# Taking q, k and v apart by tile in the latent attention's projection loop: q signals alone, and three steps change places

## The chip, the cores and the metric

The kernel runs on 1 core of one Trainium2 chip. The metric is the device time of one execution in microseconds (us). One kernel launch computes the whole model.

## The reference

Two layers over 512 tokens of width 1024. Each layer is a mixer of two attention branches, followed by a mixture of experts. The change lies in the branch with latent projections (`mla_attention`) and its hand-over to the attention loop:

```python
qb = (rmsnorm(bq, q_norm[l]) @ w_qb[l]).reshape(B, S, B_HEADS, B_NOPE_DIM + B_ROPE_DIM)
qn, qr = qb[..., :B_NOPE_DIM], qb[..., B_NOPE_DIM:]
qr = apply_rope(qr, cos[:, :, None, :], sin[:, :, None, :])
kvb = (rmsnorm(bkv, kv_norm[l]) @ w_kvb[l]).reshape(B, S, B_HEADS, B_NOPE_DIM + B_V_DIM)
kn, vb = kvb[..., :B_NOPE_DIM], kvb[..., B_NOPE_DIM:]
kr = apply_rope(bkr, cos, sin)
ob = mla_attention(qn, qr, kn, kr, vb)
gates = jax.nn.sigmoid(h @ w_gate[l] + b_gate[l])
```

`apply_rope` turns the last 32 of the 96 columns of each of the 8 heads by the angles of the token's position. `mla_attention` is a chunk-causal softmax attention over all 512 keys. The other branch, `swa_sink_attention`, is a sliding window with 2 key heads and a sink. After both, `mix = ga * (oa @ w_oa) + gb * (ob @ w_ob)` goes through `w_out` into the residual, and then 64 experts (8 groups of 8), the best 2 of the best group for each token, with D_EXPERT = 256.

## The kernel before

The program is written by hand for each engine: one block of code for SP (loads), GpSimd (POOL), ScalarE (ACT), VectorE (DVE) and TensorE (PE), and counting semaphores between them. Each engine works its own list strictly in the order written. The tokens stand in NT = 4 tiles of P = 128. The 8 PSUM banks are `ps[0]` to `ps[7]`.

A product in float32 is made of three passes (`mm3`, L1639 to L1641): the weights are split into a high part `wh` (made by ACT, L718) and a low part `wl` (made by DVE, L1120), the activations likewise. The weights come in units of up to 1 MB. `plan` lists them: units 0 to 2 and 3 to 6 are `w_in`, 7 and 8 `w_qb` (q), 9 `w_kvb` (k and v), 10 to 17 the gates (`U_G`), then `w_oa`, `w_ob`, `w_out`. `split_to(n)` on ACT and on DVE splits all units below n. SP loads a unit when its place in SBUF is free.

**The q/k/v loop** is the place of the change. On PE, for tile i (L1747 on): the product for q into banks `ps[o]` and `ps[o+1]` (18 matmuls of 384 columns), the product for k and v into `ps[o+2]` and `ps[o+3]` (12 matmuls of 512 columns), with o = 0 for even and 4 for odd tiles; then, for tile i-1, 8 transposes of q (L1780) and 8 of k (L1787) back into the same banks. Before q's product of tile i >= 2 PE waits until ACT has taken the transposed q of tile i-2 out of the banks (`qt_ev`), and before k's and v's product until DVE has taken the transposed k (`kt_ev`). The last round, i = NT, has transposes only.

- ACT, tile i: wait for the product, copy q (`qc`, L867, two), copy v (L870), then for tile i-1 copy the transposed q out (`qt`, L876, two). At i = 2 it then makes the high parts of gate unit 10 (8 instructions).
- DVE, tile i: wait for the product, copy k's part without angles (`kc`, L1291) and the shared turned part (L1293), then turn q by its angles (`rope`, L1274 to L1279, six), then for tile i-1 copy the transposed k out (`kt`, L1307, two). At i = 2 it then makes the low parts of gate unit 10 (8 instructions).

All wait for one signal a tile, which PE sets at the end of the v product:

```python
last.then_inc(S["qkv_ps" if i < NT - 1 else "unit_used"], 1)
```

PE's transposes of q of tile t wait for `q_roped`, those of k for `kn_copied`, `k_ready` and `v_copied`.

**The attention loop** follows: steps u = 0 to 63 of (query tile, head, branch). PE's step u puts out the scores of step u+1 (L1809 or L1813 for the window branch, L1818 for the latent branch), a quarter of a gate product (`gate_chunk`, from u = 1 on, L1639 to L1641, 6 matmuls), the transposes of the probabilities of step u (L1868) and the product with the values of step u-1 (L1882). DVE makes the maximum (`negm`, L1358 or L1364), ACT the exponential (L923 or L929). Before the loop ACT waits for all `kt_ev`. Before the first gate chunk PE waits for all `qt_ev` and `kt_ev`.

Of the kernel before, what the change touches and what calls it, by code (L numbers as in the profile page):

```python
# [23 lines left out]
P = 128  # L24
# [12 lines left out]
def hybrid_trunk(nc, x, positions, norm_mix, w_in, sinks, q_norm, w_qb, kv_norm, w_kvb, w_gate, b_gate,  # L37
# [3 lines left out]
    NT, KD = T // P, D // P  # L41
# [3 lines left out]
    HEADS = AH  # L45
    ROPE = IN_W - AQ - 2 * A_KV * A_DIM - QR - KVR
    HALF = ROPE // 2
# [79 lines left out]
    with ctx:  # L127
# [209 lines left out]

        block = ctx.enter_context(nc.Block())

        def dist_of(t):  # L340
# [355 lines left out]
        def _(act):  # L696
# [52 lines left out]
            for l in range(L):  # L749
# [107 lines left out]
                for i in range(NT + 1):  # L857
                    if i < NT:
                        o = 4 * (i % 2)
                        product_ready(act, "qkv_ps", i, NT, U_QKV)  # L860
                        if i >= 2:
                            act.wait_ge(S["qk_ps"], 2 * (i - 1))
                        if i == 0:
                            act.wait_ge(S["rstd2_done"], 1)
                        hh = HEADS // 2
                        for n in range(2):
                            nc.scalar.activation(qc[i % 2][:, n * hh:(n + 1) * hh, :].rearrange("p h d -> p (h d)"),  # L867
                                                 ps[o + n][:, 0:hh * QD], ACT.Copy, scale=rstd2[:, 0, i:i + 1]
                                                 ).then_inc(S["q_copied"], 1)
                        nc.scalar.activation(v[:, i, :], ps[o + 3][:, :], ACT.Copy, scale=rstd2[:, 1, i:i + 1]  # L870
                                             ).then_inc(S["v_copied"], 1)
                    if i >= 1:
                        t, o = i - 1, 4 * ((i - 1) % 2)
                        act.wait_ge(S["qk_ps"], 2 * t + 1)
                        for n in range(2):
                            nc.scalar.activation(qt[0:QD, 4 * n:4 * n + 4, t * P:(t + 1) * P],  # L876
                                                 ps[o + n][0:QD, :].rearrange("p (h q) -> p h q", h=4), ACT.Copy,
                                                 scale=B_SCALE).then_inc(S["qt_ev"], 1)
                    if i == 2:
                        split_to(U_G[0] + 1)  # L880
# [31 lines left out]

                act.wait_ge(S["kt_ev"], 2 * NT)
                act.wait_ge(S["qk_ps"], 2 * NT)
# [141 lines left out]
        def _(dve):  # L1056
# [115 lines left out]
            for l in range(L):  # L1172
# [110 lines left out]
                if l:  # L1283
                    dve.wait_ge(x_saved, l * NT * 16)
                for i in range(NT + 1):
                    if i < NT:
                        o = 4 * (i % 2)
                        product_ready(dve, "qkv_ps", i, NT, U_QKV)
                        if i >= 2:
                            dve.wait_ge(S["qk_ps"], 2 * (i - 1))  # L1290
                        V.tensor_scalar(kc[i % 2][:, :, 0:NOPE], ps[o + 2][:, :].rearrange("p (h d) -> p h d", h=HEADS),  # L1291
                                        rstd2[:, 1, i:i + 1], None, ALU.mult).then_inc(S["kn_copied"], 1)
                        V.tensor_copy(kc[i % 2][:, :, NOPE:QD],  # L1293
                                      z[:, i:i + 1, ZKR:ZC].to_broadcast([P, HEADS, ROPE])).then_inc(S["k_ready"], 1)
                        dve.wait_ge(S["q_copied"], 2 * i + 2)
                        if i:
                            dve.wait_ge(S["q_roped"], i)
                        q = qc[i % 2]
                        rope(q[:, :, NOPE:NOPE + HALF], q[:, :, NOPE + HALF:QD],
                             cos[:, i:i + 1, :].to_broadcast([P, HEADS, HALF]),  # L1300
                             sin[:, i:i + 1, :].to_broadcast([P, HEADS, HALF]),
                             [rt[:, j, :, :] for j in range(3)]).then_inc(S["q_roped"], 1)
                    if i >= 1:
                        t, o = i - 1, 4 * ((i - 1) % 2)
                        dve.wait_ge(S["qk_ps"], 2 * t + 2)
                        for n in range(2):
                            V.tensor_copy(kt[0:QD, 4 * n:4 * n + 4, t * P:(t + 1) * P],  # L1307
                                          ps[o + 2 + n][0:QD, :].rearrange("p (h q) -> p h q", h=4)
                                          ).then_inc(S["kt_ev"], 1)
                    if i == 2:  # L1310
                        split_to(U_G[0] + 1)
# [35 lines left out]
                for u in range(NUN + 1):  # L1347
                    if u < NUN:
# [13 lines left out]
                        else:  # L1362
                            dve.wait_ge(S["s_ps"], u + 1)
                            V.tensor_reduce(negm[:, t, 1, h:h + 1], ps[u % 2][:, 0:(t + 1) * P], AX, ALU.max,  # L1364
                                            negate=True).then_inc(S["negm_done"], 1)
                    w = u - 1
                    if w >= 0 and w % 2 == 1:
# [266 lines left out]
        def _(pe):  # L1634
# [17 lines left out]
            for l in range(L):  # L1652
# [99 lines left out]
                for i in range(NT + 1):  # L1752
                    if i < NT:
# [6 lines left out]
                        for half in range(2):  # L1760
                            for k in range(KQ):
                                n = n0 if k < 2 else n0 + 1
                                last = mm3(ps[o + half][:, 0:hq], ch[:, k, tok], cl[:, k, tok],
                                           *part(n, k, half * hq, hq), k == 0, k == KQ - 1)
                        if i == NT - 1:
                            last.then_inc(S["unit_used"], 2)
# [54 lines left out]
                def gate_chunk(m, i):  # L1821
                    n = U_G[0] + m // 2
                    if i == 0:
                        weights_in(n)
                        if m == 0:
                            pe.wait_ge(S["qt_ev"], 2 * NT)
                            pe.wait_ge(S["kt_ev"], 2 * NT)
                        if m >= 2:
# [19 lines left out]
                for u in range(NUN + 1):  # L1848
# [22 lines left out]
                    if w >= 0:  # L1871
                        t, h, b_ = w // (2 * HEADS), (w // 2) % HEADS, w % 2
                        nk = t + 1 if b_ else min(t + 1, 2)
                        pe.wait_ge(S["pt_dve" if b_ else "pt_act"], w // 2 + 1)
                        if w % 4 == 0 and w >= 8:
                            pe.wait_ge(S["on_done"], w // 4 - 1)
# [214 lines left out]
```

## Time and profile before

| | us |
|---|---|
| median of 3 runs | 1932.17 |
| lowest, highest | 1927.52, 1934.03 |
| the profiled execution, its time | 1933.65 |
| its span in the trace | 1931.8 |
| PE busy | 1886.8 (98% of the span), 9252 matmuls |
| DVE busy | 1437.1 (74%) |
| ACT busy | 1217.5 (63%) |
| mean granted clock of PE | 0.992 of full speed |

The chain of work that ended last lies on PE for 87% of the span, on DVE for 6%, on ACT, DMA and issue for 2% each. The granted clock is given as a share of TensorE's full speed; 0.5 is its lower level. The q/k/v loop of layer 0 lies at about 82 to 117 us of the span and that of layer 1 at about 1043 to 1078 us.

### The profile page before, as it was taken

Reading aid. Unit: us, or ns where it says so; the run is one execution under the profiler, and the core shown is the slowest. Engines: PE = TensorE matmul, PEld = TensorE weight load, DVE = VectorE, ACT = ScalarE, POOL = GpSimd, SP = SyncE. Lnnn points to the kernel's source line nnn. Section 1 sums busy time; section 2 is a strip of 40 time slices with the busy share of each in tenths; the row PEclk is TensorE's granted clock in tenths of the full one; section 3 lists DMA queues with packets and bytes.
Section 4 is the critical chain, followed back from the end, with each engine's and each line's share of the span. In section 5 each row is a group of like instructions: output and inputs, shape, how many; then the busy total and the mean of one; then the engine's idle time right before and its main releaser. Section 6 shows DMA issues by size and latency. Waiting matters only on the chain.

```text
span 1931.8 us, 27066 instructions
## 1 busy us (share of the span) xinstructions
PE 1886.8 (98%) x9252; PEld 1571.1 (81%) x9252; DVE 1437.1 (74%) x1838; ACT 1217.5 (63%) x1538; POOL 162.3 (8%) x169
## 2 busy tenths in 40 slices
PE   9999999999999999999899999999999999999997
PEld 7978878888888888888789788788888888888885
DVE  5455544589899899999834655454898999999897
ACT  5455544357777777777634655434677777777775
POOL 1000000220010011010000000002200110110000
PEclk9999999999999999999999999999999999999999
DMA  5221193499999999999612222925999999999992
GB/s 173 71 66 45 52 236 114 185 332 395 391 383 365 386 385 366 381 389 373 217 66 59 66 65 74 239 90 183 371 394 384 385 367 376 393 370 375 386 381 99
DMA packets 158791, 503.54 MB, mean 261 GB/s; under 512 B 22410, under 2 KB 38794, under 8 KB 158704
## 3 DMA queue, kind: packets, MB, share of 16 engines
q1 hardware_dynamic: 146192, 459.70, 64.2%
q0 software_dynamic: 12512, 42.69, 7.6%
q8 instruction: 53, 0.87, 0.2%
q14 instruction: 34, 0.28, 0.0%
HBM read 490.18 MB, written 32.79 MB: 271 GB/s over the span
## 4 chain that ended last, share of the span: by engine, by line
PE 87%; DVE 6%; issue 2%; ACT 2%; DMA 2%; DVEq 0%; POOL 0%; SPq 0%; ACTq 0%; POOLq 0%
PE ps L1639 25%; PE ps L1641 25%; PE ps L1640 24%; PE ps L1882 3%; DVE wl L1115 2%; PE ps L1818 2%; PE ps L1868 2%; DMA yb<-yrows 2%; PE ps L2012 1%; PE ps L1973 1%; PE ps L1927 1%; PE ps L1985 1%; PE ps L1686 1%; DVE gb L1398 1%; DVE wl L1120 1%
## 5 line engine op out<-in xcount | busy, mean ns | idle before, releaser
L1115 DVE TENSOR_TENSOR wl<-raw,wh 128x2048 fp32r<-128x2048 f32 (+1 forms) x402 | 908.5, 2280 | 154.1 <-ACT wh L717 151.8
L717 ACT ACTIVATE wh<-raw 128x2048 fp32r<-128x2048 f32 (+1 forms) x406 | 754.3, 1884 | 64.6 <-PE ps L1641 64.0
L1639 PE MATMUL ps<-wh,xgh 128*128 128x512 f32 x1024 | 412.5, 403 | 0.2
L1641 PE MATMUL ps<-wh,xgl 128*128 128x512 f32 x1024 | 400.2, 391 | 0.0
L1640 PE MATMUL ps<-wl,xgh 128*128 128x512 f32 x1024 | 399.2, 390 | 0.0
L1641 PEld LDWEIGHTS ps<-wh,xgl 128*128 128x128 f32 x1024 | 192.2, 188 | 41.8
L1639 PEld LDWEIGHTS ps<-wh,xgh 128*128 128x128 f32 x1024 | 192.3, 188 | 37.7 <-issue 2.4
L1640 PEld LDWEIGHTS ps<-wl,xgh 128*128 128x128 f32 x1024 | 192.9, 188 | 36.1
L1639 PE MATMUL ps<-wh,hth 128*128 128x512 f32 x512 | 200.2, 391 | 3.1 <-DVE htl L1170 3.1
L1641 PE MATMUL ps<-wh,htl 128*128 128x512 f32 x512 | 200.0, 391 | 0.0
L1640 PE MATMUL ps<-wl,hth 128*128 128x512 f32 x512 | 199.3, 389 | 0.0
L1011 ACT ACTIVATE hth<-ps 128x256 fp32r<-128x256 f32 x128 | 49.2, 385 | 168.2 <-PE ps L2012 168.2
L1639 PE MATMUL ps<-h1h,wh 128*128 128x512 f32 x336 | 150.6, 448 | 0.8 <-DVE h1l L1170 0.8
L1641 PE MATMUL ps<-h1h,wl 128*128 128x512 f32 x336 | 133.2, 396 | 0.0
L1640 PE MATMUL ps<-h1l,wh 128*128 128x512 f32 x336 | 133.1, 396 | 0.0
L1120 DVE SCALAR_TENSOR_TENSOR wl<-raw,gmix,wh 128x256 fp32r<-128x256 f32 (+2 forms) x192 | 86.9, 516 | 53.4 <-ACT wh L718 53.1
L1639 PEld LDWEIGHTS ps<-wh,hth 128*128 128x128 f32 x512 | 96.1, 188 | 25.4 <-issue 3.6
L1641 PEld LDWEIGHTS ps<-wh,htl 128*128 128x128 f32 x512 | 96.1, 188 | 20.3
L1640 PEld LDWEIGHTS ps<-wl,hth 128*128 128x128 f32 x512 | 96.1, 188 | 19.6
L1017 ACT ACTIVATE sgm<-ps,wslot 128x256 f32<-128x256 f32 x128 | 60.8, 475 | 77.8 <-PE ps L1641 71.7
L718 ACT ACTIVATE wh<-raw,gmix 128x256 fp32r<-128x256 f32 (+3 forms) x176 | 86.6, 553 | 26.9 <-PE ps L1641 26.9
L650 POOL TENSOR_TENSOR held<-ident 1x1 f32<-1x1 f32 x42 | 28.4, 675 | 836.3 <-DVE yb L1144 735.4
(320 smaller groups left out, 2658.6 us busy)
## 6 DMA issues: line engine op xcount, KB each, us to landing
raw<-in_w SPq DMA_DIRECT2D x512, 512.0 KB, 6.2
raw<-in_w SPq DMA_DIRECT2D x128, 1024.0 KB
raw<-in_w_gate SPq DMA_DIRECT2D x16, 1024.0 KB
xslots<-zrow POOLq DMA_DIRECT2D x2, 6240.0 KB, 36.2
raw<-in_w_out SPq DMA_DIRECT2D x8, 1024.0 KB
xg<-xslots POOLq DMA_DIRECT2D x14, 520.0 KB, 7.2
raw<-in_w_in SPq DMA_DIRECT2D x8, 800.0 KB
raw<-in_w_oa SPq DMA_DIRECT2D x4, 1024.0 KB
```

What stands on the lines that cost most here:

```text
L717: return nc.scalar.activation(dst, src, ACT.Copy)
L718: return nc.scalar.activation(dst, src, ACT.Copy, scale=k)
L1011: nc.scalar.activation(hth[:, t % 2, :, :].rearrange("p k t -> p (k t)"), ps[2][:, 0:2 * P], ACT.Copy).then_inc(S["hth_done"], 1)
L1017: nc.scalar.activation(sgm[:, e % 2, :], ps[e % 2][:, 0:FE], ACT.Silu, scale=wslot[:, 0:1]).then_inc(S["sig_done"], 1)
L1115: return V.tensor_tensor(dst, src, hi.bitcast(F32), ALU.subtract)
L1120: return V.scalar_tensor_tensor(dst, src, k, hi.bitcast(F32), ALU.mult, ALU.subtract)
L1639: MM(dst, lh, rh, start=first, stop=False)
L1640: MM(dst, lh, rl, start=False, stop=False)
L1641: return MM(dst, ll, rh, start=False, stop=last)
L1818: last = MM(dst[:, 0:n], qt[rows, h, tok], kt[rows, h, 0:n], start=True, stop=True)
L1868: last = nc.tensor.transpose(ps[3 + b_][:, k * P:(k + 1) * P], src, ident[:, :])
L1882: last = MM(ps[bank][:, o:o + VD], (ptr_b if b_ else ptr_a)[:, k * P:(k + 1) * P], val, start=(k == 0), stop=(k == nk - 1))
```

## The change

Two signals a tile take the place of one: `qkv_ps` now counts to 2 for each of the first three tiles, q and then k/v, and for the last tile `unit_used` goes up by 2 after q (as before) and by 1 after k/v, so the waits read it at two values. ACT waits for q alone before it copies q, and for k/v before it copies v. DVE turns q first and copies k behind it. ACT's high parts of gate unit 10 go from round i = 2 to round i = 1; DVE's low parts stay at i = 2. The copies of the last tile's transposed k (`keys_turned(NT - 1)`) go behind steps 0 and 1 of the attention loop on DVE. ACT no longer waits for them before the loop, and PE waits for them before the first product with values (w = 0, into bank `ps[6]`) instead of before the first gate chunk.

```diff
+        def q_ready(eng, i):
+            if i < NT - 1:
+                eng.wait_ge(S["qkv_ps"], 2 * i + 1)
+            else:
+                eng.wait_ge(S["unit_used"], U_QKV[1] - 1)
+
+        def kv_ready(eng, i):
+            if i < NT - 1:
+                eng.wait_ge(S["qkv_ps"], 2 * i + 2)
+            else:
+                eng.wait_ge(S["unit_used"], U_QKV[1])
@@ ACT, q/k/v loop
-                        product_ready(act, "qkv_ps", i, NT, U_QKV)
+                        q_ready(act, i)
...
+                        kv_ready(act, i)
                         nc.scalar.activation(v[:, i, :], ps[o + 3][:, :], ACT.Copy, scale=rstd2[:, 1, i:i + 1]
...
-                    if i == 2:
+                    if i == 1:
                         split_to(U_G[0] + 1)
...
-                act.wait_ge(S["kt_ev"], 2 * NT)
                 act.wait_ge(S["qk_ps"], 2 * NT)
@@ DVE, q/k/v loop
-                for i in range(NT + 1):
+                for i in range(NT):
                     if i < NT:
                         o = 4 * (i % 2)
-                        product_ready(dve, "qkv_ps", i, NT, U_QKV)
                         if i >= 2:
                             dve.wait_ge(S["qk_ps"], 2 * (i - 1))
+                        query_turned(i)
+                        kv_ready(dve, i)
                         V.tensor_scalar(kc[i % 2][:, :, 0:NOPE], ps[o + 2][:, :].rearrange("p (h d) -> p h d", h=HEADS),
...
                     if i >= 1:
+                        keys_turned(i - 1)
...
@@ DVE, attention loop
+                        if u == 1:
+                            keys_turned(NT - 1)
@@ PE, q/k/v loop, behind q's product
-                        if i == NT - 1:
+                        if i < NT - 1:
+                            last.then_inc(S["qkv_ps"], 1)
+                        else:
                             last.then_inc(S["unit_used"], 2)
@@ PE, gate_chunk, m == 0
                             pe.wait_ge(S["qt_ev"], 2 * NT)
-                            pe.wait_ge(S["kt_ev"], 2 * NT)
@@ PE, attention loop, product with values
+                        if w == 0:
+                            pe.wait_ge(S["kt_ev"], 2 * NT)
```

`query_turned(i)` holds the waits for `q_copied` and `q_roped` and the call of `rope` as they stood, `keys_turned(t)` the wait for `qk_ps` and the two copies of transposed k.

The order of DVE from round i = 3 to step 2 of the attention loop, layer 0. `kc` is the copy of k, `qc` the copy of q that is turned, `kt` the transposed k, `wl` the low parts of gate unit 10, `negm` and `sa` belong to the softmax steps. Before:

```order
L1120 SCALAR_TENSOR_TENSOR wl_219<-raw_205,gmix,wh_227 128x256 x8
L1291 TENSOR_SCALAR kc_118<-ps,rstd_74 128x8x64
L1293 COPY kc_118<-z 128x8x32
L1274 TENSOR_TENSOR rt<-qc_116,cos 128x128
...
L1279 TENSOR_TENSOR qc_116<-rt 128x8x16
L1307 COPY kt<-ps 96x4x128 x4
L1356 COPY sa<-nsink 128x1
L1358 ISA sa,negm<-ps,dist,nsink 128x128
L1358 ISA negm 128x1
L1364 TENSOR_REDUCE negm<-ps 128x1
```

With the change:

```order
L1132 SCALAR_TENSOR_TENSOR wl_219<-raw_205,gmix,wh_227 128x256 x8
L1286 TENSOR_TENSOR rt<-qc_116,cos 128x128
...
L1291 TENSOR_TENSOR qc_116<-rt 128x8x16
L1323 TENSOR_SCALAR kc_118<-ps,rstd_74 128x8x64
L1325 COPY kc_118<-z 128x8x32
L1312 COPY kt<-ps 96x4x128 x2
L1375 COPY sa<-nsink 128x1
L1377 ISA sa,negm<-ps,dist,nsink 128x128
L1377 ISA negm 128x1
L1383 TENSOR_REDUCE negm<-ps 128x1
L1312 COPY kt<-ps 96x4x128 x2
```

The six turns of q stand ahead of the two copies of k, and of the four copies of transposed k two now stand behind the first two softmax steps.

The order of ACT in rounds i = 1 and i = 2, layer 0 (`qc` copies of q, `v` the copy of v, `qt` the transposed q, `wh` the high parts of gate unit 10). Before:

```order
L867 ACTIVATE qc_116<-ps,rstd_74 128x384 x2
L870 ACTIVATE v<-ps,rstd_74 128x512
L876 ACTIVATE qt<-ps 96x4x128 x2
L867 ACTIVATE qc_115<-ps,rstd_74 128x384 x2
L870 ACTIVATE v<-ps,rstd_74 128x512
L876 ACTIVATE qt<-ps 96x4x128 x2
L718 ACTIVATE wh_227<-raw_205,gmix 128x256 x8
```

With the change:

```order
L879 ACTIVATE qc_116<-ps,rstd_74 128x384 x2
L883 ACTIVATE v<-ps,rstd_74 128x512
L889 ACTIVATE qt<-ps 96x4x128 x2
L730 ACTIVATE wh_227<-raw_205,gmix 128x256 x8
L879 ACTIVATE qc_115<-ps,rstd_74 128x384 x2
L883 ACTIVATE v<-ps,rstd_74 128x512
L889 ACTIVATE qt<-ps 96x4x128 x2
```

The 8 instructions of the gate unit now stand ahead of tile 2's q copies.

## Rows read from the trace of the kernel before

**Rows 1.** Waits of PE over the whole span: total us, times, longest us.
```profile
PE ps L1639 <- ACT qt L876: 3.7, 4, 0.9
PE ps L1868 <- ACT sa L923: 3.0, 2, 1.5
PE ps L1780 <- DVE qc L1279: 2.7, 2, 1.4
```

**Rows 2.** Windows: length, busy us per engine, granted PE clock, DMA share, GB/s.
```profile
120.00:124.00 4.00, 4.00 (x15) 3.09 (x14) 0.83 (x4) 1.98 (x6) 0.00 (x0) 0.60 0.01 4
...
250.00:330.00 80.00, 77.59 (x388) 64.08 (x387) 33.76 (x60) 32.00 (x48) 3.45 (x4) 0.96 0.67 181
330.00:960.00 630.00, 626.20 (x2920) 515.03 (x2919) 547.84 (x484) 441.63 (x382) 72.64 (x57) 1.00 0.92 345
```

**Rows 3.** Timeline of PE: start, us, instruction [idle before it, releaser]; last two: layer 1.
```profile
94.16 1.04 PE L1780 MATMUL ps<-ident,qc 128*96 128x128 f32 x8
95.03 1.04 PE L1787 MATMUL ps<-ident,kc 128*96 128x128 f32 x8
97.00 0.45 PE L1639 MATMUL ps<-wh,ch 128*128 128x384 f32 x1 [0.93 <-ACT qt L876]
...
100.23 0.39 PE L1639 MATMUL ps<-wh,ch 128*128 128x512 f32 x1
...
102.99 1.04 PE L1780 MATMUL ps<-ident,qc 128*96 128x128 f32 x8
...
105.83 0.44 PE L1639 MATMUL ps<-wh,ch 128*128 128x384 f32 x1 [0.93 <-ACT qt L876]
...
115.09 1.08 PE L1780 MATMUL ps<-ident,qc 128*96 128x128 f32 x8 [1.36 <-DVE qc L1279]
...
116.97 0.48 PE L1809 MATMUL ps<-ak,aq 64*128 64x128 f32 x2
117.39 0.49 PE L1818 MATMUL ps<-kt,qt 100*128 100x128 f32 x2
119.35 0.33 PE L1868 MATMUL ps<-ident,sa 128*128 128x128 f32 x1 [1.48 <-ACT sa L923]
...
1079.99 0.33 PE L1868 MATMUL ps<-ident,sa 128*128 128x128 f32 x1 [1.48 <-ACT sa L923]
...
1082.27 0.33 PE L1882 MATMUL ps<-av,ptr_a 128*128 128x64 f32 x2
```

**Rows 4.** Timeline of ACT, layer 0.
```profile
94.36 1.05 ACT L867 ACTIVATE qc<-ps,rstd 128x384 f32<-128x384 f32 x2 [4.29 <-PE ps L1641]
95.30 0.69 ACT L870 ACTIVATE v<-ps,rstd 128x512 f32<-128x512 f32 x1
95.87 1.07 ACT L876 ACTIVATE qt<-ps 96x512 f32<-96x512 f32 x2
...
105.66 3.31 ACT L718 ACTIVATE wh<-raw,gmix 128x256 fp32r<-128x256 f32 x8
...
118.81 0.40 ACT L923 ACTIVATE sa<-sa,negm 128x129 f32<-128x129 f32 x1 [1.52 <-DVE negm L1358]
```

**Rows 5.** Timeline of DVE, layer 0.
```profile
109.01 3.25 DVE L1120 SCALAR_TENSOR_TENSOR wl<-raw,gmix,wh 128x256 fp32r<-128x256 f32 x8 [1.62 <-ACT wh L718]
112.18 0.75 DVE L1291 TENSOR_SCALAR kc<-ps,rstd 128x512 f32<-128x512 f32 x1
...
113.11 0.29 DVE L1274 TENSOR_TENSOR rt<-qc,cos 128x128 f32<-128x128 f32 x1
...
117.08 1.28 DVE L1307 COPY kt<-ps 96x512 f32<-96x512 f32 x2 [0.85 <-PE ps L1787]
...
118.35 0.34 DVE L1358 CUSTOM_DVE_ANT_0 sa<-ps,dist,nsink 128x128 f32<-128x128 f32 x1
```

**Rows 6.** DMA over 70 to 125 us in 40 slices of 1.375 us: busy tenths, GB/s.
```profile
DMA  0000000028924300000000000000049999100000
GB/s 0 0 0 0 0 0 0 0 69 245 374 75 78 18 0 0 12 0 0 0 0 0 0 0 0 0 0 0 0 94 354 364 352 328 32 6 12 0 0 0
```

More of the change, by code:

```diff
@@ L1284, in _, with query_turned, keys_turned @@
                     dve.wait_ge(x_saved, l * NT * 16)
-                for i in range(NT + 1):
+                def query_turned(i):
+                    dve.wait_ge(S["q_copied"], 2 * i + 2)
+                    if i:
+                        dve.wait_ge(S["q_roped"], i)
+                    q = qc[i % 2]
+                    rope(q[:, :, NOPE:NOPE + HALF], q[:, :, NOPE + HALF:QD],
+                         cos[:, i:i + 1, :].to_broadcast([P, HEADS, HALF]),
+                         sin[:, i:i + 1, :].to_broadcast([P, HEADS, HALF]),
+                         [rt[:, j, :, :] for j in range(3)]).then_inc(S["q_roped"], 1)
+                def keys_turned(t):
+                    o = 4 * (t % 2)
+                    dve.wait_ge(S["qk_ps"], 2 * t + 2)
+                    for n in range(2):
+                        V.tensor_copy(kt[0:QD, 4 * n:4 * n + 4, t * P:(t + 1) * P],
+                                      ps[o + 2 + n][0:QD, :].rearrange("p (h q) -> p h q", h=4)
+                                      ).then_inc(S["kt_ev"], 1)
+                for i in range(NT):
                     if i < NT:
                         o = 4 * (i % 2)
-                        product_ready(dve, "qkv_ps", i, NT, U_QKV)
                         if i >= 2:
                             dve.wait_ge(S["qk_ps"], 2 * (i - 1))
+                        query_turned(i)
+                        kv_ready(dve, i)
                         V.tensor_scalar(kc[i % 2][:, :, 0:NOPE], ps[o + 2][:, :].rearrange("p (h d) -> p h d", h=HEADS),
@@ L1294, in _ @@
                                       z[:, i:i + 1, ZKR:ZC].to_broadcast([P, HEADS, ROPE])).then_inc(S["k_ready"], 1)
[L1295 to L1302, printed above, removed]
-                    if i >= 1:
[L1304 to L1309, printed above, removed]
+                    if i >= 1:
+                        keys_turned(i - 1)
                     if i == 2:
```

## The prediction

> **What bounds the kernel now.** I read the waits of PE first, since PE is busy for 98% of the span and a change can only pay where PE stands. The q/k/v loop and its hand-over show there with three groups [rows 1]: PE waits 4 times, up to 0.9 us each, until ACT has copied a transposed q out; twice, 1.4 us, for the turned q of the last tile; and twice, 1.5 us, for the first exponential of the attention loop. With two layers that is 0.93 + 0.93 + 1.36 + 1.48 = 4.7 us a layer. The timeline of PE shows where they lie in layer 0 [rows 3]. Behind the loop everything hangs on PE: the experts' stretch has 626.20 us of PE work in 630 us, with DMA at a share of 0.92 [rows 2], so a mixer that ends sooner should move all that follows. The loads of that stretch are released by PE's progress and move with it.
>
> Last, the granted clock. In the window 120 to 124 us it is 0.60 [rows 2]; between the levels 1.0 (2.4 GHz) and 0.5 (1.2 GHz) that is 0.8 of 4 us at the lower one, 3.2 us, and work there takes double, so 1.6 us are lost. It follows directly on the 1.48 us wait at 119.35. Layer 1 has the same wait at 1079.99 [rows 3] and no fall behind it: its first product with values comes 2.28 us later, at 1082.27.
>
> **The change part by part**, for layer 0; layer 1 has the same rows.
>
> *The two waits for transposed q.* ACT finds q ready only at 94.36, with the whole product, then copies q (to 95.30), v (to 95.87) and only then the transposed q, 1.07 us, and PE goes on at 97.00 [rows 3, 4]. With its own signal q is ready one k/v product earlier; that product is 102.99 - 100.23 = 2.76 us long [rows 3], the copies of q take 95.30 - 94.36 = 0.94 us, so they vanish under it. v then starts at 94.36 and takes 95.87 - 95.30 = 0.57 us, to 94.93. PE's q transposes end at 94.16 + 1.04 = 95.20; ACT can begin there, not sooner. 95.20 + 1.07 and about 0.1 of hand-over make 96.37 in place of 97.00: 0.63 us gained for tile 2. PE's k transposes end at 95.03 + 1.04 = 96.07, so about 0.3 us of the wait stays. Tile 3 repeats it: it starts at 105.83 - 1.26 = 104.57.
>
> *ACT's gate unit a round sooner* costs nothing by this account. It takes 3.31 us [rows 4], now from about 96.4 to 99.7. q of tile 2 is ready 100.23 - 97.00 = 3.23 us after the tile's start, at 99.6, so its copies are hardly held up; PE needs tile 2's turned q only behind tile 3's products, and ACT's next task for PE, v and the transposed q, comes at 102.4. If that cover went, the 3.31 us would stand before `qt`. The move matters for the last tile: where it stood, at 105.66, it would now reach into the wait for tile 3's q. Its raw weights must have landed; see the last rival.
>
> *The turned q of the last tile.* Before, DVE starts the two copies of k at 112.18 and the angles at 113.11; PE gets its q at 115.09 [rows 3, 5]. Now q of tile 3 is ready at 104.57 + 3.23 + 0.15 = 107.95 and copied by 108.9. DVE is the later one by a hair: it copies transposed k of tile 1 when PE's transposes end (104.3), 1.28 us, then the low parts of gate unit 10, 3.25 us [rows 5], to 108.85. Angles then take 115.09 - 113.11 = 1.98 us, to about 111.0, and the k copies 0.93 us more, to 111.9. PE by its own work: products 102.99 - 97.00 = 5.99 us, transposes of tile 2 2 x 0.88 us, so it asks for the turned q at 104.57 + 7.75 = 112.3 and for k at 113.2. Both have 1.3 us to spare. The wait of 1.36 us goes, and with it 0.15 us of restart: 105.83 + 7.75 = 113.58 against 115.09, 1.5 us gained. From here the k copies are behind the angles; late next would be k, with that 1.3 us.
>
> *The entry of the attention loop.* PE's transposes of tile 3 and first scores follow at 112.3 + 1.75 = 114.05 (before: 116.97). Before, the softmax step had to let the last keys' copies go first: they start at 117.08 and take 1.28 us, the step starts at 118.35, ACT at 118.81, PE at 119.35 [rows 3 to 5]. Now the scores are there 0.5 us after their start, at 114.55; 118.81 - 118.35 = 0.46 us and 119.35 - 118.81 = 0.54 us later PE goes on, at 115.6. Second scores end at 114.05 + 0.42 + 0.49 = 115.0, so 0.6 us of the 1.48 stay, 0.9 gained. The moved copies cost DVE 1.28 us, from 115.3 to 116.6; PE asks for them before its first product with values, 2.28 us behind 115.6, at 117.9 (the distance in layer 1). The new wait is covered by 1.3 us. Behind it on PE's list stands everything; but DVE has nothing ahead of those copies that PE has not delivered. The next maximum needs scores of about 116.4, so it is late by some 0.2 us, with the whole gate quarter (1.4 us) over it.
>
> *Not on the path:* the new signals and waits are a few in each layer on engines that stand idle at that point; no row prices them, so between 0 and the 0.1 us of a hand-over each I take 0. SP's wait for q of the last tile moves forward by 1.3 us, and nothing needs those loads for several us.
>
> **The sum.** Per layer 0.63 + 0.63 + 1.5 + 0.9 = 3.7 us (119.35 less 115.6 gives the same), for both 7.4 us. The clock fall of layer 0, 1.6 us, follows on a wait that shrinks from 1.48 to 0.6 us with no other wait of over 0.3 us ahead of it; I take it as gone. Against the profiled execution's own 1933.65 us: 1933.65 - 7.4 - 1.6 = 1924.7. That execution is 1.5 us above the median of the runs shown; a run without the fall would gain only the 7.4. Between 1924.7 and the median's 1932.17 - 7.4 = 1924.8, less half a fall for the median (one layer of two had it), 1924.0, I forecast **1924.3 us**, 0.41% less.
>
> Its ends: the restart rests of 0.3 us may be 0 or stay as they were, 0.93 (2 x 1.26 us); the fall may leave or stay (1.6 us); and the window 250 to 330 us has 0.96 [rows 2], or 6.4 us at the lower level, 3.2 us lost, which a shift of 4 us may lengthen or halve. The runs shown already spread from 1927.52 to 1934.03.
>
> **Rivals.**
> 1. *The clock fall does not leave, or another comes.* For it: the same 1.48 us wait is followed by a fall in one layer and not in the other, so the wait's length alone does not decide. Against it: no wait of that size stays here. It gives 1933.65 - 7.4 = 1926.2. The Trainium skill, page "TensorE: Matmul & The Clock Gate", Part 1, says that the gate's window is free-running and does not reset when a kernel starts, so where idle time falls decides. By that rule the 1.6 us are luck of the placing; the trace agrees in that two equal waits of 1.48 us end differently.
> 2. *DVE, not the signal, holds the last angles.* The low parts of the gate unit still stand ahead of them and end only 0.1 us before q's copies. If that block is more than 1.3 us later than I have it, the 1.5 us go back: 1933.65 - 2 x 2.2 - 1.6 = 1927.6. Against it: the high parts that it needs are ready at about 99.7, six us before.
> 3. *The gain is taken back later*, by a transfer or an engine that does not move with PE: 1932. Against it speaks 626.20 of 630 us.
> 4. *Slower: ACT is held by the gate unit's raw weights.* They are loaded in two bursts, 81 to 88 us (1 MB) and 110 to 117 us (2 MB) [rows 6], and the first is unit 10 if the loads go in the order of the list. The worst that the rows allow is that it has just landed at 105.66, where ACT starts without a wait [rows 4]. Then ACT stands from 96.4, ends at 108.97, copies q, v and transposed q of tile 2 by 108.97 + 0.94 + 0.57 + 1.07 = 111.6, and tile 3 starts 5.9 us later than before; the later gains, 1.5 + 0.9, leave 3.5 us of loss a layer: 1933.65 + 7 = 1940.6. It decides against the change if the weights land later than about 102, and the first burst says 88.
>
> **How the numbers follow.** What a measurement of this kernel can tell from no change is about 0.3%, 5.8 us, so the bound for faster is 1926.4. Forecast 0.68, of which 0.05 ends above the bound by the spread of runs; rival 1 0.16 (0.10 below, 0.06 above); rival 2 0.08 (0.01 and 0.07); rival 3 0.04; rival 4 0.04. So faster 0.74, same 0.22, slower 0.04. The range goes from 1919.5 (forecast less the distance of the lowest run from the median, 4.7) to 1928.5 (rival 2 with 1 us of spread).
>
> **What would show it.** Right: PE's waits on `qt` at about 0.3 us, none on the last turned q, 0.6 us before the first exponential's transposes, no wait of PE on `kt` at its first product with values, ACT's gate unit starting right behind the transposed q of tile 0, and the distance from PE's first latent q product to the first exponential's transposes shorter by 3.7 us in both layers. Wrong: a wait of ACT before the gate unit, a wait of PE on k's copies (DVE late), a `kt` wait at the first product with values, or a clock below 1.0 in the loop. The forecast fails if the two distances shrink and the span does not.

## The result and the profile after

| | before | after |
|---|---|---|
| median (lowest to highest), us | 1931.88 (1925.38 to 1934.03), 9 runs | 1920.59 (1919.11 to 1923.07), 9 runs |
| profiled execution, us | 1933.65 | 1920.6 |
| its span, us | 1931.8 | 1918.7 |
| its mean granted PE clock | 0.992 | 0.993 |

The ratio after to before is 0.9942 with a 95% interval of 0.9932 to 0.9951: 0.58% faster. The prediction said 1924.3 us, 0.41% faster. The way and the range were right, the size was too small: 7.9 us less than the 1932.17 us known then, where 11.3 us less than 1931.88 us was measured.

The waits of PE over the whole span of the changed kernel (total us, times, longest us); they answer to [rows 1]. The lines have moved: the transposes of q and k stand in L1803 and L1810, those of the probabilities in L1890, the passes of a product in L1660 to L1662.

```profile
PE ps L1707 <- issue: 5.8, 1, 5.8
PE ps L1890 <- ACT pr L941: 3.0, 2, 1.5
PE ps L1836 <- DVE qs L1182: 2.8, 2, 1.4
PE ps L1660 <- DVE htl L1182: 2.3, 3, 1.0
...
PE ps L1890 <- ACT sa L935: 1.2, 2, 0.6
PE ps L1660 <- ACT qt L889: 1.2, 4, 0.3
PE ps L2036 <- DVE hw L1605: 1.1, 2, 0.6
```

The waits for transposed q went from 0.93 to 0.3 us, the one before the first exponential's transposes from 1.48 to 0.6 us, and the wait for the turned q of the last tile is not in the list. The second and third line are waits inside the attention loop that the change leaves as they were: for the last exponential (`pr`) and for the low part of the rows (`qs`). Its timeline of PE, in layer 0 and then in layer 1 [rows 3]:

```profile
94.10 1.04 PE L1803 MATMUL ps<-ident,qc 128*96 128x128 f32 x8
...
102.31 1.03 PE L1803 MATMUL ps<-ident,qc 128*96 128x128 f32 x8
...
112.27 1.04 PE L1803 MATMUL ps<-ident,qc 128*96 128x128 f32 x8
113.14 1.04 PE L1810 MATMUL ps<-ident,kc 128*96 128x128 f32 x8
114.11 0.48 PE L1832 MATMUL ps<-ak,aq 64*128 64x128 f32 x2
114.52 0.49 PE L1841 MATMUL ps<-kt,qt 100*128 100x128 f32 x2
115.63 0.33 PE L1890 MATMUL ps<-ident,sa 128*128 128x128 f32 x1 [0.62 <-ACT sa L935]
117.92 0.33 PE L1906 MATMUL ps<-av,ptr_a 128*128 128x64 f32 x2
...
1050.01 0.44 PE L1660 MATMUL ps<-wh,ch 128*128 128x384 f32 x1 [0.29 <-ACT qt L889]
...
1058.22 0.44 PE L1660 MATMUL ps<-wh,ch 128*128 128x384 f32 x1 [0.29 <-ACT qt L889]
...
1069.34 0.33 PE L1890 MATMUL ps<-ident,sa 128*128 128x128 f32 x1 [0.62 <-ACT sa L935]
```

From the q transposes of tile 0 to the transposes of the first exponential it took 119.35 - 94.16 = 25.19 us and takes 115.63 - 94.10 = 21.53 us: 3.66 us less, 3.7 predicted; in layer 1, from 25.19 to 21.54 us. The first product with values, where the wait for the last keys now stands, comes 2.29 us later with no wait. What lies behind it on DVE:

```profile
105.46 3.25 DVE L1132 SCALAR_TENSOR_TENSOR wl<-raw,gmix,wh 128x256 fp32r<-128x256 f32 x8
109.10 0.29 DVE L1286 TENSOR_TENSOR rt<-qc,cos 128x128 f32<-128x128 f32 x1 [0.39 <-issue]
...
110.94 0.74 DVE L1323 TENSOR_SCALAR kc<-ps,rstd 128x512 f32<-128x512 f32 x1
...
114.63 0.35 DVE L1377 CUSTOM_DVE_ANT_0 sa<-ps,dist,nsink 128x128 f32<-128x128 f32 x1 [0.26 <-PE ps L1832]
...
115.26 1.27 DVE L1312 COPY kt<-ps 96x512 f32<-96x512 f32 x2
```

The low parts of the gate unit end at 108.7, ACT's copies of q only at 109.0, so it is q that comes last here, and not DVE's block as the prediction had it "by a hair". The angles start at 109.10, copies of k follow, the softmax step starts with the scores at 114.63 (before: 118.35, behind the copies), and the last keys are copied behind it [rows 5]. ACT makes the high parts right behind the transposed q of tile 0, without a wait for their weights [rows 4]:

```profile
95.17 1.08 ACT L889 ACTIVATE qt<-ps 96x512 f32<-96x512 f32 x2 [0.19 <-PE ps L1803]
96.14 3.30 ACT L730 ACTIVATE wh<-raw,gmix 128x256 fp32r<-128x256 f32 x8
```

The two layers are 7.3 of the 13.1 us between the two spans. The windows show a part of the rest, the granted clock. After, first at the entry of the attention loop of layer 0, then at the end of that loop in both layers, then the experts' stretch (the columns are those of [rows 2]):

```profile
116.00:120.00 4.00, 4.00 (x22) 3.26 (x22) 1.50 (x7) 2.71 (x9) 0.00 (x0) 1.00 0.02 4
270.00:285.00 15.00, 13.42 (x67) 11.32 (x67) 5.32 (x12) 3.31 (x8) 3.44 (x4) 0.77 0.66 231
...
1225.00:1240.00 15.00, 12.46 (x63) 9.79 (x62) 5.35 (x10) 3.35 (x9) 3.46 (x4) 0.89 0.96 261
330.00:950.00 620.00, 616.65 (x2878) 507.18 (x2877) 539.94 (x471) 437.01 (x375) 70.47 (x57) 1.00 0.93 350
```

and the same place at the end of the loop of layer 1 in the kernel before:

```profile
1235.00:1250.00 15.00, 13.46 (x66) 11.37 (x65) 5.86 (x12) 2.76 (x8) 3.46 (x4) 0.77 0.90 239
```

The fall at the entry of layer 0 (0.60 over 4 us [rows 2]) is gone. At the end of the loop in layer 1 a clock of 0.77 over 15 us, 6.9 us at the lower level of 0.5, became 0.89, 3.3 us. At that level each microsecond costs half of one, since matmuls of 512 columns start 0.43 us apart there and 0.23 us apart at full clock: 1.6 us at the entry and 1.8 us at the end. By the starts of the same matmuls in both traces it is 1.5 us and 1.1 us; with 7.3 us that makes 9.9 of 13.1 us. By the same starts 1.8 us more went at the hand-over between the layers, where PE's long wait went from 6.2 to 5.8 us and the clock over 940 to 1050 us is 0.97 in both. The last 1.3 us went in the experts' stretch of layer 1; over the whole span PE's waits for split activations and hidden rows (`htl`, `hw`) are 3.1 + 1.4 us before and 2.3 + 1.1 us after. These are single profiles, and the clock part of them is a draw: a second profile of the same changed kernel (e11) has no fall at the end of layer 1's loop.

### The profile page after: what moved, and what is told of

Same layout as the page of the kernel before. It is cut to its first block, busy times and chain, and to the rows that moved or that the text cites. A ratio compares the mean times of both kernels' runs of the same rounds, so it can differ in the third digit from the quotient of the medians.

```text
span 1918.7 us, 27064 instructions
## 1 busy us (share of the span) xinstructions
PE 1881.6 (98%) x9252; PEld 1567.4 (82%) x9252; DVE 1436.6 (75%) x1838; ACT 1218.7 (64%) x1538; POOL 161.2 (8%) x169
## 4 chain that ended last, share of the span: by engine, by line
PE 91%; DVE 4%; issue 2%; ACT 1%; DMA 1%; DVEq 0%; SPq 0%; POOL 0%; ACTq 0%; POOLq 0%
PE ps L1660 26%; PE ps L1662 26%; PE ps L1661 26%; PE ps L1906 3%; PE ps L1841 2%; PE ps L1890 2%; PE ps L2036 1%; DVE wl L1127 1%; PE ps L1997 1%; PE ps L1951 1%; PE ps L2009 1%; PE ps L1707 1%; DVE gb L1419 1%; DVE ml L1182 1%; PE ps L1836 0%
## 5 line engine op out<-in xcount | busy, mean ns | idle before, releaser
L1660 PE MATMUL ps<-wh,xgh 128*128 128x512 f32 x1024 | 412.3, 403 | 0.1
L1662 PE MATMUL ps<-wh,xgl 128*128 128x512 f32 x1024 | 400.1, 391 | 0.0
L1662 PEld LDWEIGHTS ps<-wh,xgl 128*128 128x128 f32 x1024 | 192.2, 188 | 41.6
L1660 PEld LDWEIGHTS ps<-wh,xgh 128*128 128x128 f32 x1024 | 192.3, 188 | 37.5 <-issue 2.2
L1660 PE MATMUL ps<-wh,hth 128*128 128x512 f32 x512 | 200.2, 391 | 2.3 <-DVE htl L1182 2.3
L1662 PE MATMUL ps<-wh,htl 128*128 128x512 f32 x512 | 199.9, 390 | 0.0
L1660 PE MATMUL ps<-h1h,wh 128*128 128x512 f32 x336 | 150.1, 447 | 0.8 <-DVE h1l L1182 0.8
L1662 PE MATMUL ps<-h1h,wl 128*128 128x512 f32 x336 | 133.1, 396 | 0.0
L1660 PEld LDWEIGHTS ps<-wh,hth 128*128 128x128 f32 x512 | 96.1, 188 | 24.5 <-issue 3.8
L1662 PEld LDWEIGHTS ps<-wh,htl 128*128 128x128 f32 x512 | 96.1, 188 | 20.3
L941 ACT ACTIVATE pr<-ps,negm 128x128 f32<-128x128 f32 (+3 forms) x64 | 33.7, 527 | 101.1 <-DVE negm L1383 101.1
```

What stands on the lines that cost most here:

```text
L1660: MM(dst, lh, rh, start=first, stop=False)
L1662: return MM(dst, ll, rh, start=False, stop=last)
```

## The experiments

Theory A is the account of the prediction: waits of PE, each term by its own mechanism, and what goes beyond them is the granted clock. The rivals stand with each run. e1 to e4 take one step of the change back. All times are medians, and "over the changed kernel" means over its 1920.59 us. The runs fall into four groups taken one after the other on several chips: the result above, e1 to e4, e5 to e8, e9 to e11. The kernel before ran in each; its means are 1931.0, 1931.5, 1931.0 and 1931.2 us, so times of different groups can be compared to about half a microsecond. The mean granted clock of a run is given where it matters; what 0.001 of it is worth is worked out behind e4.

### e1: ACT's gate unit back in its old round

```diff
-                    if i == 1:
+                    if i == 2:
                         split_to(U_G[0] + 1)
```

> The changed kernel with ACT's high parts of gate unit 10 back in round i = 2. Theory A, the prediction's own words (the move matters by ACT's own queue): ACT works on the unit from about 104.4 to 107.7 us and q of tile 3 is ready at 107.9, so nothing is lost and the time is that of the changed kernel, 1920.6 us. Theory B (the move matters by DVE's low parts, which wait for the high parts): DVE starts them at 107.7 in place of 105.5 and ends at 110.9, the angles of tile 3 end at 112.9 where PE asks at 112.3, so PE waits about 0.65 us a layer on the turned q and the time is some 1.4 us above the changed kernel's.

Measured: 1924.72 us (1921.67 to 1925.66, 7 runs). The timeline of ACT, of DVE, then that of PE:

```profile
104.62 3.30 ACT L730 ACTIVATE wh<-raw,gmix 128x256 fp32r<-128x256 f32 x8
108.21 1.05 ACT L879 ACTIVATE qc<-ps,rstd 128x384 f32<-128x384 f32 x2 [0.28 <-PE ps L1662]
```
```profile
107.96 3.26 DVE L1132 SCALAR_TENSOR_TENSOR wl<-raw,gmix,wh 128x256 fp32r<-128x256 f32 x8 [2.15 <-ACT wh L730]
```
```profile
113.11 1.08 PE L1803 MATMUL ps<-ident,qc 128*96 128x128 f32 x8 [0.42 <-DVE qc L1291]
...
115.25 0.46 PE L1832 MATMUL ps<-ak,aq 64*128 64x128 f32 x2 [0.20 <-DVE kt L1312]
```

Theory B holds in its mechanism and the prediction's reason falls. ACT is done with the unit before q of tile 3 is there and still waits 0.28 us for it. DVE waits 2.15 us for the high parts and is late with all that follows: PE waits 0.42 us on the turned q and 0.20 us on the transposed k of tile 2, a wait I had not named. The distance from tile 0's q transposes to the first exponential's is 116.75 - 94.38 = 22.37 us, 0.84 more a layer than after. The size was missed: 4.1 us over the changed kernel where theory B said 1.4. The distances give 1.7 us of it; the mean clock of these runs is 0.9933 against 0.9946 of the changed kernel's, about 1.8 us. In this profile the clock fell at the entry of layer 0 again:

```profile
117.00:122.00 5.00, 5.00 (x19) 4.03 (x19) 1.61 (x8) 2.73 (x10) 0.00 (x0) 0.66 0.02 3
```

### e2: k copied ahead of the angles

```diff
-                        query_turned(i)
                         kv_ready(dve, i)
...
                                       z[:, i:i + 1, ZKR:ZC].to_broadcast([P, HEADS, ROPE])).then_inc(S["k_ready"], 1)
+                        query_turned(i)
```

> The changed kernel with DVE's two copies of k ahead of the angles again (and so the wait for k/v ahead of them). Theory A (the order on DVE carries most of the last tile's gain): k/v of tile 3 is ready at 110.7 us, copies to 111.65, angles to 113.6, PE waits 1.35 us a layer on the turned q, 2.7 us in all over the changed kernel. Theory B (the separate signal for q alone carries it): PE waits at most 0.3 us and the time stays within 1 us of the changed kernel.

Measured: 1923.30 us (1921.59 to 1924.66, 6 runs). PE's timeline:

```profile
114.09 1.08 PE L1803 MATMUL ps<-ident,qc 128*96 128x128 f32 x8 [1.20 <-DVE qc L1291]
```

Theory A: the wait of the last tile is back with 1.20 us (1.35 expected), and the time is 2.7 us over the changed kernel. While k stands ahead of the angles, the other steps take no more than 0.16 us off that wait of 1.36 us. The mean clock is 0.9950, no lower than the changed kernel's: beside its own length this wait of 1.2 us shows no cost in clock.

### e3: the last keys copied first

```diff
+                keys_turned(NT - 1)
...
-                        if u == 1:
-                            keys_turned(NT - 1)
```

> The changed kernel with the copies of the last transposed k ahead of the first softmax step again. Theory A: PE's wait before the first exponential's transposes goes from 0.6 to 1.5 us, 0.9 us a layer, 1.8 us in all plus now and then a fall of the clock (up to 1.7 us each). Theory B (the step waits for the scores anyway): PE's wait stays near 0.6 us, no difference.

Measured: 1925.06 us (1920.87 to 1926.97, 9 runs), 4.5 us over the changed kernel.

```profile
116.18 0.33 PE L1889 MATMUL ps<-ident,sa 128*128 128x128 f32 x1 [1.46 <-ACT sa L935]
```

The wait is as theory A has it, 1.46 us, 0.84 more a layer. But 1.7 us of waits brought 4.5 us of time: the mean clock is 0.9923 against 0.9946, about 3.3 us. In this profile the clock falls behind that wait in layer 1, seen in its window:

```profile
1068.00:1078.00 10.00, 8.54 (x35) 6.68 (x35) 3.23 (x14) 5.49 (x20) 0.00 (x0) 0.83 0.17 52
```

### e4: ACT waits for the whole product again

```diff
-                        q_ready(act, i)
+                        kv_ready(act, i)
```

> The changed kernel with ACT waiting for the whole product before it copies q. Theory A: the two waits of 0.93 us for transposed q come back (0.63 us each), the angles of tile 3 end about 2.7 us later and PE waits about 1.4 us for them, 2.75 us a layer, 5.5 us in all; only the 0.9 us a layer of the entry stays, so the time is about 1926. Theory B (the four steps overlap and any three give the gain): under 2 us over the changed kernel.

Measured: 1926.44 us (1924.99 to 1932.29, 12 runs).

```profile
96.68 0.44 PE L1660 MATMUL ps<-wh,ch 128*128 128x384 f32 x1 [0.93 <-ACT qt L889]
...
114.83 1.08 PE L1803 MATMUL ps<-ident,qc 128*96 128x128 f32 x8 [1.41 <-DVE qc L1291]
...
116.97 0.46 PE L1832 MATMUL ps<-ak,aq 64*128 64x128 f32 x2 [0.20 <-DVE kt L1312]
```

Theory A: 0.93 us twice and 1.41 us are back, and the time is 5.9 us over the changed kernel, 5.5 expected; by the distances it is 6.2 us. With angles first but q late, DVE is 0.2 us late with a transposed k as well.

### The clock term, from runs that change nothing

Each execution reports the mean granted clock of its span. Beside e1 to e4, e5 to e8, and e9 to e11 the kernel before ran 53 times. Its time goes with that clock:

```
clock   runs   mean us
0.990      3   1935.13
0.991     17   1933.30
0.992     11   1932.22
0.993      7   1930.11
0.994      7   1929.44
0.995      4   1928.08
0.996      2   1925.78
0.997      2   1924.90
```

A straight line through the 53 runs falls by 1.42 us for each 0.001 (correlation -0.96), near to what half speed costs: 0.001 of the mean clock is 3.9 us of the 1932 us at the lower level of 0.5, and 1.9 us lost. Part of them cost nothing: in the trace of the kernel before the clock is 0.53 over 1925 to 1931.8 us, where PE has no matmul left. The mean clock of the kernel before is 0.9925, that of the changed kernel 0.9943 in its first 9 runs and 0.9946 with the 5 of e11. So far the clock and the time only go together; e5, e9 and e10 act on this term.

### e5: the kernel before with its wait filled

```diff
+                        if u == 0:
+                            for _ in range(5):
+                                MM(ps[3][:, :], upper_r[:, :], upper_r[:, :].rearrange("p (o q) -> p o q", o=1)
+                                   .to_broadcast([P, 4, P]), start=True, stop=True)
                         pe.wait_ge(S["exp_done"], u + 1)
```

> The kernel before with 5 matmuls of 128x512 on constants put on PE into the wait of 1.48 us ahead of the first exponential's transposes (bank ps[3], which is overwritten next); nothing is shortened. Theory A (the part of the gain above the 7.4 us of waits is the granted clock, and falls behind the wait at the entry of the attention loop are a piece of it): the distances of the loop stay as in the kernel before, no fall begins behind that wait in either layer, the mean granted clock goes from about 0.992 up by some 0.0004 to 0.0009 and the median falls by 1 to 2 us, to about 1930. Theory B (the rest of the gain comes from the experts' stretch or the loads): no difference, or up to 0.4 us slower for matmuls that reach past the wait.

Measured: 1928.45 us (1924.84 to 1932.46, 12 runs) against 1931.37 for the kernel before beside it, ratio 0.9988 (0.9977 to 0.9999); mean clock 0.9943 against 0.9926. All waits of the loop are as before but for the filled one, of which 0.31 us are left, and the distance from tile 0's q transposes is 25.24 us, as before. Its windows: the entry of layer 0, the end of the attention loop of layer 0, then of layer 1.

```profile
116.00:126.00 10.00, 9.69 (x53) 7.48 (x52) 3.43 (x16) 6.91 (x22) 0.00 (x0) 1.00 0.09 29
275.00:290.00 15.00, 13.10 (x60) 10.66 (x60) 5.23 (x10) 2.63 (x7) 3.44 (x4) 0.77 0.97 264
1234.00:1249.00 15.00, 12.23 (x69) 10.14 (x68) 5.07 (x8) 5.54 (x8) 3.46 (x4) 1.00 1.01 262
```

Theory A, and above the size it gave (1 to 2 us; 0.0004 to 0.0009 of clock, 0.0017 measured): useless work in one wait of 1.48 us a layer buys 2.4 us by the means and 2.9 us by the medians. The interval of the ratio allows anything from 0.2 to 4.4 us. The profile also has no fall at the end of the loop of layer 1, some 160 us behind the filled wait. That is a draw and not the filling: two profiles of the changed kernel differ in the same way (see e10).

### e6, e7 and e8: two waits that the change leaves

```diff
@@ e6, DVE
-                    if u in (12, 15, 23, 24, 39, 40):
+                    if u in (12, 13, 23, 24, 39, 40):
@@ e7, DVE
-                    if u % 8 in (5, 6):
+                    if u % 8 in (5, 6) and u < NUN - 2:
                         split_half(U_G[0] + u // 8 + 1, u % 8 - 5)
+                    if u == NUN:
+                        split_half(U_G[0] + NUN // 8, 1)
```

> The changed kernel with DVE's low part of the second key head's rows of query tile 1 at step u = 13 in place of 15. PE waits 1.4 us a layer there. Theory A (DVE's place in its list is what is late): the wait goes, 2.8 us less, about 1917.8. Theory B (the rows from ACT or DVE's load at step 13, which then holds 0.7 + 1.7 us in a step of 2.1 us, are what is late): another wait of 0.5 to 1.5 us comes in its place on the scores or the transposed probabilities of steps 13 to 15, under 1 us less.

> The changed kernel with DVE's second half of the low parts of unit 18 (1.22 us) moved from step 62 behind step 64's copy. PE waits 1.5 us a layer for the last exponential, and the granted clock falls behind that wait in both layers (6.8 and 3.4 us at the lower level in the profile). Theory A: the wait shrinks by 1.2 us a layer, 2.4 us, and with it falls get rarer, up to 1.7 us for each 3.4 us at the lower level: 2.4 to 7 us less than the changed kernel, 1914 to 1918. Theory B (the last exponential or its copies are bound by something else): the wait stays over 1 us and the time within 1 us of 1920.6.

> The changed kernel with both edits, the rows at step 13 and the low half behind step 64. If the two are apart in time, their gains add: 2.8 + 2.4 = 5.2 us by the waits and up to 3 us by the clock, 1912 to 1915.5. If the clock only moves its falls elsewhere, 1915.5 or a little more.

Measured: e6 1918.00 us (1916.20 to 1919.36, 6 runs); e7 1915.02 us (1913.81 to 1917.38, 6 runs); e8 1911.89 us (1911.42 to 1912.65, 5 runs), ratio to the kernel before 0.9902 (0.9888 to 0.9916). In e6 and e8 the wait of 1.4 us for the rows' low part has left PE's list and no other came near it. PE's waits in e8, of which the last was 1.5 us a layer after the change:

```profile
PE ps L1892 <- ACT sa L935: 1.2, 2, 0.6
PE ps L1662 <- ACT qt L889: 1.2, 4, 0.3
...
PE ps L1892 <- ACT pr L941: 1.1, 2, 0.5
```

e7's windows at the end of the attention loop, in both layers:

```profile
265.00:285.00 20.00, 18.20 (x106) 14.81 (x105) 9.02 (x18) 7.42 (x16) 3.44 (x4) 1.00 1.00 273
1215.00:1235.00 20.00, 18.46 (x113) 15.19 (x111) 9.03 (x18) 7.09 (x18) 3.46 (x4) 1.00 1.00 271
```

e6 gives 2.6 us for 2.8 us of waits (2.8 expected). Its mean clock is 0.9937, not above the changed kernel's 0.9946: taking away this wait of 1.4 us shows no gain in clock. e7 takes 1.9 us of waits and gives 5.6 us of time with a mean clock of 0.9962, and its profile has no fall at the loop's end. e8 (0.9964) is the fastest kernel of the study, 8.7 us under the changed one.

### e9: the last keys' step alone, on the kernel before

```diff
+                        if u == 1:
+                            keys_turned(NT - 1)
...
-                            pe.wait_ge(S["kt_ev"], 2 * NT)
...
+                        if w == 0:
+                            pe.wait_ge(S["kt_ev"], 2 * NT)
```

(ACT's wait for the last keys is gone too, and the copies are taken out of the loop's last round.)

> The kernel before with one step of the change alone: the last transposed k's copies behind softmax steps 0 and 1, with the waits that belong to it. Theory A (each 0.9 us of this wait carries a clock term with it): PE's wait before the first exponential's transposes goes from 1.48 to about 0.6 us in both layers, 1.8 us, and the mean clock rises as when that wait was filled (about 0.0017, at some 1.5 us for each 0.001, 2.5 us): 4 to 4.5 us less than the kernel before, about 1927, with the two waits for transposed q (0.93 us) and for the turned q (1.36 us) unchanged. Theory B (waits only): 1.8 us less, about 1929.5.

Measured: 1926.08 us (1923.64 to 1928.28, 11 runs), beside 1932.49 us for the kernel before, ratio 0.9974 (0.9964 to 0.9984); mean clock 0.9945 against 0.9924. Its waits of PE:

```profile
PE ps L1643 <- ACT qt L876: 3.7, 4, 0.9
...
PE ps L1784 <- DVE qc L1278: 2.7, 2, 1.4
...
PE ps L1871 <- ACT sa L922: 1.2, 2, 0.6
```

Theory A. One moved pair of copies takes 1.8 us of waits away and brings 5.1 us on the means of the runs (1931.19 less 1926.08; 6.4 us on the medians, 4 to 4.5 us expected); by the line above 0.0021 of clock is 3.0 us of it.

### e10 and e11: the last wait filled, and the change again

e10 puts the 5 matmuls of e5 into the changed kernel at `u == NUN - 1`, in `ps[4]`. e11 is the changed kernel.

> The changed kernel with 5 matmuls of 128x512 on constants in PE's 1.5 us wait before the last exponential's transposes (bank ps[4], overwritten next); nothing is shortened. Theory A: the falls at the end of the attention loop go or halve, the mean clock rises by about 0.0015 to 0.002 over the changed kernel's 0.9943, and the time falls by 2 to 3.5 us, to 1917 to 1918.5. Theory B (falls there come from the thin work around the wait, not from the wait): the falls stay, time within 1 us of the changed kernel.

> The changed kernel once more, on the chip and in the rounds of the other two. Both theories: a median of 1920 to 1921.5 us and a mean clock of 0.994 to 0.9945; the runs of the kernel before beside it about 1931.5 us and 0.9925.

Measured: e10 1918.13 us (1917.43 to 1919.35, 5 runs), mean clock 0.9962; e11 1919.83 us (1918.51 to 1920.94, 5 runs), mean clock 0.995. In e10 the end of the loop runs at full clock in both layers:

```profile
268.00:288.00 20.00, 18.46 (x104) 14.93 (x103) 8.81 (x16) 8.05 (x14) 3.44 (x4) 1.00 0.97 266
1222.00:1242.00 20.00, 18.45 (x106) 15.11 (x105) 8.77 (x15) 9.15 (x15) 3.46 (x4) 1.00 1.01 269
```

and the same windows of e11:

```profile
268.00:288.00 20.00, 17.96 (x88) 14.51 (x86) 7.84 (x16) 4.59 (x12) 3.45 (x4) 0.83 0.92 265
1222.00:1242.00 20.00, 17.24 (x98) 13.93 (x98) 8.59 (x17) 7.50 (x14) 3.46 (x4) 1.00 0.94 268
```

e10 is 1.7 us under e11 by the medians, 1.4 us by the means, and 2.5 us under the first runs of the change. Theory A gave 2 to 3.5 us, theory B under 1 us; with 5 runs each the time alone decides weakly for A. The clock helps: 0.9962 is what e7 has, where the same wait was shortened. In the profiles the end of layer 0's loop tells the kernels apart. All ten profiles with the wait of 1.5 us have a fall there, a clock of 0.86 to 0.93 over 265 to 290 us; e10 and e7 have 1.00, e8 with its shortened wait 0.93. So the falls there hang mostly on the wait and not on the thin work around it. Layer 1 tells nothing: only five of the same ten have a fall at its loop's end, and e11 has none where the first profile of the same kernel had 0.89.

### All by waits and clock

Mean time of each kernel, brought to the clock 0.9925 by 1.42 us for each 0.001; beside it what the distances in the traces give for both layers. The 53 runs of the kernel before have a mean of 1931.25 us.

```
kernel                mean us   clock    at 0.9925   less than before   by the traces
after (9 + 5 runs)    1920.27   0.9946   1923.2      8.0                7.3
e1 gate unit late     1924.23   0.9933   1925.4      5.9                5.6
e2 k ahead            1923.31   0.9950   1926.9      4.4                4.5
e3 keys first         1924.89   0.9923   1924.6      6.6                5.6
e4 one signal         1927.40   0.9942   1929.8      1.4                1.1
e5 before, filled     1928.58   0.9943   1931.1      0.1                0
e6 rows low sooner    1918.00   0.9937   1919.7      11.6               10.1
e7 low half later     1915.20   0.9962   1920.5      10.8               9.2
e8 both               1911.90   0.9964   1917.4      13.8               12.0
e9 keys alone         1926.08   0.9945   1928.9      2.3                1.6
e10 after, filled     1918.29   0.9962   1923.5      7.7                7.3
```

(e6, e7 and e8: 7.3 us and the 2.8, 1.9 and 4.7 us of waits that left PE's list.) The two columns agree within 1 us up to e5 and in e9 and e10; e6 to e8 gained 1.5 to 1.8 us more than waits and clock give, and that is open.

The column of the clock shows something that no single run does: what a wait costs in clock depends on its place. (The standard error of each mean clock is 0.0002 to 0.0006.) Where the entry of the attention loop has its full wait (before 1.48 us, e3 1.46 us) the mean clock is 0.9925 and 0.9923. Where that wait is 0.6 us or filled, it is 0.9942 to 0.9950 in the changed kernel, e2, e4, e5 and e9, although e2 and e4 have a wait of 1.2 and 1.4 us for the last turned q, a few microseconds ahead. e9 alone has the whole clock term of the change. e1 seems to lie between, 0.9933, with waits of 0.42, 0.20 and 0.62 us close together. The wait at the end of the loop costs clock too (e7, e8 and e10 have 0.9962 to 0.9964), that for the rows does not measurably (e6). Why these two places and not the others was not tried.

## Why the prediction was right, and what it mis-sized

- *The two waits for transposed q*: 0.63 us each, rest 0.3 us. Measured rest 0.29 us in both layers. Right, and e4 brings the 0.93 us back.
- *The turned q of the last tile*: PE was to ask at 112.3 and did at 112.27, without a wait. That the order on DVE and the separate signal are both needed is shown by e2 (1.20 us) and e4 (1.41 us).
- *The entry*: 115.6 predicted, 115.63 measured; 0.6 us of the wait stay, 0.62 measured. Shown by e3 and e9: e3 takes this step alone back, e9 makes it alone.
- *The new wait of PE on the last keys*: no wait in the profile, the copies ran from 115.26 to 116.5. Right.
- *ACT's gate unit a round sooner*: right that it costs nothing and that its weights had landed (rival 4: 96.14 without a wait). The reason for its use was wrong. The prediction said that "where it stood, at 105.66, it would now reach into the wait for tile 3's q". e1 shows that it is DVE's low parts that wait for it, 2.15 us, and through them the angles and a transposed k. A chain over two engines was read as one engine's queue, although rival 2 names the link ("the high parts that it needs").
- *The sum of waits*, 7.4 us: 7.3 us by the distances of both layers, and e3, e4 and e9 split it as stated, to within 0.4 us a layer. Rivals 2 to 4 fell.
- *The clock* is the term that was mis-sized. The prediction took "half a fall for the median", 0.8 us, from one profile that had one fall in two layers. Measured: the mean clock rose from 0.9925 to 0.9946 over 14 runs, by 1.42 us for each 0.001 about 2.9 us. 7.3 + 2.9 = 10.2 of the 11.0 us between the means. The place was right, the entry of the attention loop: e9, with that step alone, has the whole rise. A profile holds one draw of the falls, and half a fall read from one draw was too little. Rival 1, that the falls are luck of the placing and do not leave, is wrong as a forecast of the mean: each profile places them differently, but how often they come depends on the waits at the loop's entry and end (e3, e5, e9, e10). The Trainium skill, page "TensorE: Matmul & The Clock Gate", Part 1, says that the gate's window is free-running; the traces agree in so far as two profiles of the changed kernel have 0.89 and 1.00 at the same place.
- *A sign of being wrong that did come*: the prediction's list has "a clock below 1.0 in the loop". The changed kernel has 0.77 over 270 to 285 us, at the end of layer 0's loop, with a wait of 1.5 us that was there before and that the prediction did not read. It had seen only the 0.96 over 250 to 330 us and put it in the range. e7 and e10 show that this too could be won.
- *A slip in the range*: 1924.3 less 4.7 is 1919.6 us, not 1919.5. It changes nothing.
- *What stays open*: 0.8 us of the means, within their scatter; 1.5 to 1.8 us in e6 to e8; and in the profile 1.8 us at the hand-over and 1.3 us in the experts' stretch of layer 1. PE's waits for split activations there (`htl`) vary between 2.0 and 2.6 us among the profiles of the other kernels, e5 and e9 with 2.1 and 2.3 us among them, so 3.1 us in the one profile of before is probably a draw too. This was not tried.

## What to carry to other kernels

Where an engine is busy for 98% and its lower clock level costs double, a wait of 1.5 us can be worth more than 1.5 us: at the entry of the attention loop 1.7 us of waits came with 3 us of clock, while waits of 1.2 to 1.4 us at two other places (e2, e6) showed none. So ask it of each wait by itself, with the mean granted clock over many runs, not with the falls that one profile happens to hold. If such a wait cannot be shortened, work that nobody reads, put into it, won 2.4 us and 1.4 us here by the means (e5, e10). When a step is moved ahead on one engine, follow its product to the engine that consumes it: the use of the gate unit's move lay in DVE's list, not in ACT's.

## What the runs showed of the hardware that was not expected

- One and the same program's time follows its mean granted clock with -0.96 over 53 runs, from 1935.1 us at 0.990 to 1924.9 us at 0.997; almost the whole spread of this kernel on one core is this.
- At the entry of the attention loop a wait of 1.5 us of PE, in each of two layers, goes with 0.002 of mean clock, about 3 us (before, e3 against the changed kernel, e9), and matmuls on constants in it bring the clock back (e5). A wait of 1.2 us, 3.4 us ahead of it, shows no such cost (e2: 0.9950).
- The kernels with the highest mean clock also spread less, though fewer runs span less by themselves: 1911.42 to 1912.65 us in e8's 5 runs, 1919.11 to 1923.07 after the change in 9, 1925.38 to 1934.03 before in 9.
